# One pipeline of 16 attention units in place of 12 and 4, with the second kind's transposed operands in free ring places

## The reference

```python
o_n = nsa_mixer(q_n, k_c, v_c, k_s, v_s, k_w, v_w, g_n, ...)   # 8 query heads in 2 key groups, 3 gated branches
o_m = moba_mixer(q_m, k_m, v_m, cos, sin)                      # 8 heads with keys of their own
o = jnp.concatenate([o_n, o_m], axis=-1) @ w_o[l]
```

## Time and profile before

| | us |
|---|---|
| median of 3 runs | 2891.91 (2890.43 to 2893.74) |
| the profiled execution | 2889.56 |
| span of the profiled execution | 2887.8 |
| mean granted PE clock | 0.979 |
| PE, PEld, DVE, ACT, POOL busy in the span | 2796.0, 2382.1, 1772.7, 1317.6, 172.1 |

### The profile page before, as it was taken

The page is one execution under the profiler, slowest core; times in us unless marked ns, Lnnn a source line. Parts: engine busy times, 40 slices in busy tenths (PEclk is TensorE's granted clock), DMA queues, the critical chain, the costliest instruction groups (busy, mean ns, idle before and its releaser), DMA issues.

```text
span 2887.8 us, 35130 instructions
## 1 busy us (share of the span) xinstructions
PE 2796.0 (97%) x13510; PEld 2382.1 (82%) x13510; DVE 1772.7 (61%) x2028; ACT 1317.6 (46%) x1658; POOL 172.1 (6%) x132
## 2 busy tenths in 40 slices
PE   8998999999999999999999999998889999999998
PEld 8998978888878888888888889876778888888886
DVE  4466568676557787865555564444684755644445
ACT  5454234454434545434454444344455444344443
POOL 0001620000000000000000002630000000000000
PEclk9998999999999999999999999897999999999999
DMA  8453038877647777775555556450455766755553
GB/s 283 150 171 119 0 124 290 286 274 266 217 161 255 281 273 261 283 252 199 190 188 197 185 179 202 160 190 1 154 201 186 267 227 218 275 188 179 190 187 119
DMA packets 293266, 579.60 MB, mean 201 GB/s; under 512 B 9168, under 2 KB 46192, under 8 KB 292112
## 3 DMA queue, kind: packets, MB, share of 16 engines
q1 hardware_dynamic: 291296, 566.08, 57.5%
q0 software_dynamic: 1120, 8.57, 0.8%
q10 hardware_dynamic: 720, 3.15, 0.3%
HBM read 575.66 MB, written 2.10 MB: 200 GB/s over the span
## 4 chain that ended last, share of the span: by engine, by line
PE 94%; DVE 3%; ACT 1%; issue 1%; DMA 0%; POOL 0%; SPq 0%; DVEq 0%; ACTq 0%
PE GP L853 28%; PE GP L855 28%; PE GP L854 28%; PE TA L830 2%; PE TB L476 2%; PE TB L830 1%; PE GP L462 1%; PE TA L1210 1%; PE TB L872 1%; DVE small L553 0%; PE GP L1056 0%; PE TA L1056 0%; PE GP L1046 0%; DMA x<-in_x 0%; PE TA L1244 0%
## 5 line engine op out<-in xcount | busy, mean ns | idle before, releaser
L1754 DVE TENSOR_TENSOR wlo<-raw,whi 128x1024 fp32r<-128x1024 f32 (+2 forms) x904 | 1086.9, 1214 | 853.6 <-ACT whi L1286 844.7
L1286 ACT CAST whi<-raw 128x1024 fp32r<-128x1024 f32 (+2 forms) x904 | 924.8, 1029 | 1206.7 <-PE GP L855 1158.5
L853 PE MATMUL GP<-whi,hhi 128*128 128x512 f32 (+2 forms) x1792 | 689.4, 385 | 3.1 <-DVE hlo L578 1.6
L855 PE MATMUL GP<-whi,hlo 128*128 128x512 f32 (+2 forms) x1792 | 681.3, 380 | 0.0
L854 PE MATMUL GP<-wlo,hhi 128*128 128x512 f32 (+2 forms) x1792 | 681.2, 380 | 0.0
L853 PEld LDWEIGHTS GP<-whi,hhi 128*128 128x128 f32 x1792 | 338.7, 189 | 54.7 <-issue 3.0
L855 PEld LDWEIGHTS GP<-whi,hlo 128*128 128x128 f32 x1792 | 338.1, 189 | 52.0
L854 PEld LDWEIGHTS GP<-wlo,hhi 128*128 128x128 f32 x1792 | 338.4, 189 | 51.1 <-issue 1.0
L853 PE MATMUL GP<-whi,bhi 128*128 128x512 f32 x704 | 276.6, 393 | 0.2 <-DVE blo L1814 0.2
L1742 DVE SCALAR_TENSOR_TENSOR ada_acc<-raw,csig,ada_acc 128x512 f32<-128x512 f32 x360 | 270.2, 751 | 10.2
L855 PE MATMUL GP<-whi,blo 128*128 128x512 f32 x704 | 274.3, 390 | 0.0
(11 more groups left out here) (410 smaller groups left out, 2667.7 us busy)
## 6 DMA issues: line engine op xcount, KB each, us to landing
raw<-in_w_up SPq DMA_DIRECT2D x108, 1024.0 KB, 5.3
raw<-in_w_down SPq DMA_DIRECT2D x108, 1024.0 KB, 5.1
raw<-in_w_ada SPq DMA_DIRECT2D x96, 1024.0 KB, 5.1
raw<-in_w_gate SPq DMA_DIRECT2D x44, 1024.0 KB, 5.1
raw<-in_w_in SPq DMA_DIRECT2D x48, 856.0 KB, 4.6
raw<-in_w_xkv SPq DMA_DIRECT2D x32, 1024.0 KB, 5.5
raw<-in_w_in SPq DMA_DIRECT2D x24, 1024.0 KB, 4.9
raw<-in_w_in SPq DMA_DIRECT2D x24, 864.0 KB, 4.5
```

Source lines behind the costliest of these rows:

```text
L853: pe.matmul(o, ahi[:, kt, t], whi[r][:, k, 0:q.width], start=first, stop=False)
L855: m = pe.matmul(o, alo[:, kt, t], whi[r][:, k, 0:q.width], start=False, stop=last)
L1286: nc.scalar.copy(whi[(2 * g + s) % NRING][:, :, 0:q.width], raw[j % NSLOT][:, 2 * s:2 * s + 2, 0:q.width])\
L1754: TTo(wlo[r][:, :, 0:q.width], raw[j % NSLOT][:, 2 * s:2 * s + 2, 0:q.width], whi[r][:, :, 0:q.width].bitcast(F32), ALU.subtract).then_inc ...
```

## The change

The 12 and 4 units become one list of 16, run as one pipeline `natt`; stage `matt` is gone. The three blocks of n2 are transposed at points of `w_in2c` (behind its third, fifth and seventh unit), and ACT copies them in hooks. The second kind gets operands of its own, `qTm` and `kTm`, of 8 KB per partition each, which lie over `whi2`, `whi3` and `wlo2`, `wlo3`. Its four blocks are transposed behind `w_in2c` (two) and behind the transposes of units 0 and 1 (one each). So that the ring places are free, `w_in2c` splits only the first unit of `w_oa` ahead (`lead=1`), and the second is split when attention is over.

```diff
-                   for i, (n, u, g) in enumerate((("xatt", 0, 0), ("natt", 2, 8), ("matt", 14, 12)))}
+                   for i, (n, u, g) in enumerate((("xatt", 0, 0), ("natt", 2, 8)))}
...
+        qTm = nc.alloc_sbuf_tensor_at("qTm", [P, 8, T], F32, offset=ring0 + 4096 * 2)
+        kTm = nc.alloc_sbuf_tensor_at("kTm", [P, 8, T], F32, offset=ring0 + 4096 * (NRING + 2))
...
-                                   qk=[[(qT2[:, h, hf * P:hf * P + P], kT2[:, h, 0:nk * P])] for h in hs],
+                                   qk=[[(qTm[:, h, hf * P:hf * P + P], kTm[:, h, 0:nk * P])] for h in hs],
...
-        def attention_pe(pe, turn, nm_, us):
+        def attention_pe(pe, turn, nm_, us, behind={}, ahead={}):
...
+                if i in ahead:
+                    ahead[i]()
...
                     if ngroup >= 2:
                         pe.wait_ge(*N(nm_, "lo", ngroup - 1))
+                    elif nm_ == "natt":
+                        pe.wait_ge(*N("m2", "c", 4))
...
                 m.then_inc(N(nm_, "t")[0], 1)
+                if i in behind:
+                    behind[i]()
                 if i:
                     values(i - 1)
...
-            product(PH["w_in2c"], hhi, hlo, lambda u: (S("norm_lo"), 40))
-
+            def later_turn(g):
+                if g == 0:
+                    pe.wait_ge(S("rope_done"), 2)
+                elif g == 1:
+                    pe.wait_ge(S("cmp_oc"), 2)
+                else:
+                    pe.wait_ge(*N("n2", "c", 1))
+                turn_in2(turn, "n2", later[g])
+
+            def block_turn(g):
+                if g == 0:
+                    pe.wait_ge(*N("n2", "c", 3))
+                elif g == 1:
+                    pe.wait_ge(*N("n2", "c", 2))
+                else:
+                    pe.wait_ge(*N("m2", "c", g))
+                turn_in2(turn, "m2", blocks[g])
+
+            product(PH["w_in2c"], hhi, hlo, lambda u: (S("norm_lo"), 40),
+                    points={(0, 2): lambda: later_turn(0), (1, 0): lambda: later_turn(1), (1, 2): lambda: later_turn(2)})
+            pe.wait_ge(S("rope_done"), 4)
+            block_turn(0)
+            block_turn(1)
             for e in range(2):
                 pe.wait_ge(S(f"evac{e}"), 1 + PH["w_in2c"].ev1)
...
-            turn_in2(pe, turn, "n2")
-            attention_pe(pe, turn, "natt", nsa_units())
-            turn_in2(pe, turn, "m2")
-            attention_pe(pe, turn, "matt", moba_units())
-            pe.wait_ge(*N("natt", "lo", 4))
+            attention_pe(pe, turn, "natt", nsa_units() + moba_units(), behind={0: lambda: block_turn(2), 1: lambda: block_turn(3)},
+                         ahead={12: lambda: pe.wait_ge(*N("m2", "c", 4))})
...
                 for j in range(LEAD):
-                    if nxt is not None:
+                    if nxt is not None and j < lead:
                         split_hi(*nxt, j)
...
+            for g, at in enumerate((5, 7, 9)):
+                hooks[at] = hooks.get(at, []) + [lambda it, g=g: turn_in2_act(act, "n2", later[g], g + 1)]
+            phase(PH["w_in2c"], hooks, lead=1)
+            turn_in2_act(act, "m2", blocks[0], 1)
+            turn_in2_act(act, "m2", blocks[1], 2)
+            attention_act(act, "natt", nsa_units() + moba_units(),
+                          behind={i: lambda i=i: turn_in2_act(act, "m2", blocks[2 + i], 3 + i) for i in range(2)})
+            split_hi(PH["w_oa"], 0, 1)
...
-            phase(PH["w_in2c"], {})
+            phase(PH["w_in2c"], {}, lead=1)
...
-            attention_dve(dve, link, "natt", nsa_units())
-            dve.wait_ge(*N("m2", "c", 4))
-            dve.sem_inc(N("matt", "go")[0], 1)
-            attention_dve(dve, link, "matt", moba_units())
+            attention_dve(dve, link, "natt", nsa_units() + moba_units())
+            split_lo(PH["w_oa"], 0, 1)
```

More of the change, by code:

```diff
@@ L488, in attention_pe @@
                     pe.wait_ge(*N(nm_, "c", i))
+                elif nm_ == "natt":
+                    pe.wait_ge(*N("m2", "c", 1))
                 for kb in range((u["L"] + P - 1) // P):
@@ L496, in attention_pe, with attention_act @@
             values(len(us) - 1)
-        def attention_act(act, nm_, us):
+        def attention_act(act, nm_, us, behind={}):
             ng = 0
@@ L596, in GP_flat, with turn_in2, turn_in2_act @@
             return _F()
[L600 to L612, removed]
-                    pe.wait_ge(*N("natt", "lo", 4))
[L614 to L623, removed]
+        later = [(qT2, 0, [0, 128, 256, 384], TA), (qT2, 4, [512, 640, 768, 896], TB),
+                 (kT2, 0, [KV0 + 512, KV0 + 640, KV0 + 1024, KV0 + 1152], TA)]
+        blocks = [(qTm, 0, [QM0 + P * i for i in range(4)], TA), (qTm, 4, [QM0 + P * i for i in range(4, 8)], TB),
+                  (kTm, 0, [QM0 + 1024 + P * i for i in range(4)], TB), (kTm, 4, [QM0 + 1024 + P * i for i in range(4, 8)], TB)]
+        def turn_in2(turn, nm_, part):
+            _, _, cs, tp = part
+            for f, c in enumerate(cs):
+                for h in range(NH):
+                    m = turn(tp[:, f * T + h * P:f * T + h * P + P], p2[:, h, c:c + P])
+            m.then_inc(N(nm_, "t")[0], 1)
+        def turn_in2_act(act, nm_, part, n):
+            dst, a, _, tp = part
+            act.wait_ge(*N(nm_, "t", n))
+            nc.scalar.copy(dst[:, a:a + 4, :], v(tp, T)).then_inc(N(nm_, "c")[0], 1)
         raws = [(x, 0, hhi, hlo), (memt, 2, mhi, mlo), (x, 1, hhi, hlo), (x, 3, bhi, blo)]
@@ L1245, in gate_row @@
                     .then_inc(S("gate_mm"), 1)
-            product(PH["w_oa"], hhi, hlo, lambda u: N("matt", "lo", 4),
+            product(PH["w_oa"], hhi, hlo, lambda u: N("natt", "lo", 8),
                     points={divmod(i + 1, 4): lambda i=i: gate_row(0, i) for i in range(4)})
-            product(PH["w_ob"], hhi, hlo, lambda u: N("matt", "lo", 4))
+            product(PH["w_ob"], hhi, hlo, lambda u: N("natt", "lo", 8))
             for g in range(6):
@@ L1287, in split_hi, with body @@
                         .then_inc(S("hi_done"), 1)
-            def body(q, it, nxt, hooks):
+            def body(q, it, nxt, hooks, lead=LEAD):
                 g = 0
@@ L1305, in body, with phase @@
                         f(it)
-            def phase(q, hooks, peel=False, last={}, ahead=True, head={}):
+            def phase(q, hooks, peel=False, last={}, ahead=True, head={}, lead=LEAD):
+                assert lead == LEAD or q.n == 1
                 i0 = order.index(q)
@@ L1318, in phase @@
                     with loop(act, m) as it:
-                        body(q, it, (q, it + 1), hooks)
+                        body(q, it, (q, it + 1), hooks, lead)
                 if not same:
                     both = {at: hooks.get(at, []) + last.get(at, []) for at in hooks.keys() | last.keys()}
-                    body(q, q.n - 1, (nq, 0) if nq is not None else None, both)
+                    body(q, q.n - 1, (nq, 0) if nq is not None else None, both, lead)
             def raw_square(s, hs=(0, 1)):
@@ L1780, in body, with phase @@
                     ada_out()
-            def phase(q, hooks, peel=False, links=0, last={}, ahead=True, head={}):
+            def phase(q, hooks, peel=False, links=0, last={}, ahead=True, head={}, lead=LEAD):
+                assert lead == LEAD or q.n == 1
                 i0 = order.index(q)
```

4 lines of the change are left out of this document (removed).

## The result

The changed kernel takes 2872.84 us (median of 4, 2870.88 to 2874.52), the kernel before 2891.17 (median of 4): ratio 0.9938, 95% interval 0.9925 to 0.9950, so 18.3 us less. 2874.0 was forecast, with 2867 to 2881 as the range.

What follows compares the result with a forecast made beforehand. PE was taken as the bound, busy 2796.0 of 2887.8 us, with this stage bound by the PE, DVE, ACT chain. Front 1.5, seam 15.8 and clock gave gains of 13.0 to 23.6; 18 was taken: 2874 us, range 2867 to 2881.

Steps and rivals of the forecast that it cites:

- The front: From `w_in2c` to the first exponentials: three blocks go under the product; 1.5 us gained, bounds 2.1 gain to 0.4 loss.
- The seam: Values of unit 11 to transposes of the second new unit: only unit 15's scores remain, 17.6 us become 1.8, removing 15.8.
- The tail: Transposes of the second new unit to `w_oa`: 13.8 us, same order of work, about 3 us wait at unit 14; nothing gained.
- low piece of the old tail: Half-clock work in the tail before `w_oa` that need not come again; 1.7 us given back.
- The clock: PE's granted clock around the seam decides the rest; a shorter low stretch than before was assumed, total gain 18 us.
- two ends: Clock at the seam: low as before from unit 11's transposes gives 13.0 us gain; full gives 21.9, or 1.7 more.
- price of 0.45 us for a low microsecond: Within the half-clock rival: each added microsecond of half clock in the stage loses 0.45 us.
- Half clock all along: Rival: clock stays at 0.50 from behind the front to `w_oa`, which starts 12 us later; 2904 us; chance 0.04.
- Full clock through the seam: Rival: denser work keeps PE at full clock at the seam; gain 21 to 24 us, 2868 to 2871; chance 0.2.
- The start of `w_oa`: Second unit split behind attention, ready 2.5 us into `w_oa`, needed after 5.4; no cost.
- Both margins: At `w_oa`: the late `w_ada` load is used 16.5 us in, and the `w_o` loads come 2.5 us later; no cost.

Runs made afterwards that it cites:

- first profile: The changed kernel as first measured and profiled, against the kernel before: 2872.84 us, ratio 0.9938.
- filled kernel before: The kernel before with discarded matmuls of constants put into nine of PE's waits for a division, against the kernel before: 2885.20 us, ratio 0.9980.
- second profile: The changed kernel measured and profiled again without any edit, against the kernel before: 2871.36 us, ratio 0.9930.
- seam alone: The changed kernel with the three n2 blocks transposed behind `w_in2c` instead of inside it, against the kernel before: 2872.22 us, ratio 0.9940.
- six `pT`: The changed kernel with six buffers `pT` instead of three, the new ones in `p2`; against the kernel before: 2866.80 us, ratio 0.9925.
- changed kernel with filling: The changed kernel with discarded matmuls of constants in PE's waits at seven units, against the kernel before: 2867.41 us, ratio 0.9919.

## Why the prediction was right

**The front.** Forecast: `w_in2c` 2.6 us longer on PE, scores 2.1 us earlier, exponentials 1.5. Measured from the base: the last matmul of `w_in2c` starts at 44.86 instead of 42.14 (2.7), scores at 46.83 instead of 49.14 (2.3), exponentials 1.51 earlier. That the two blocks behind units 0 and 1 fit into gaps at nothing holds at full clock only. From the first exponentials to the transposes of unit 6 it took 23.0 us in the first profile, with nothing low, and 23.0 in the filled kernel before, which has no blocks there (3.4 low). With 6.8 low us there it took 25.6 in the second profile and in the seam alone, against 24.1 before with 10.2 low: at half clock PE has no gap left, and the blocks cost 1.4 us or more. Ahead of the scores they cost 5.0 us, so their place is still worth more than the 1.9 of the forecast. What the front brings to the time is small: 1.3 us alone and 0.9 as the last piece, neither told apart from nothing.

**The seam.** Forecast: 17.6 us become 1.8. Measured: 2014.57 - 2013.01 = 1.6. This is the step that carries the result, and the seam alone gave it.

**The tail.** Forecast: 13.8 us, with a wait of about 3 us at unit 14. Measured: 2028.68 - 2014.57 = 14.1, wait 3.08. The reason given was only half of it: behind the copy of unit 12 the cast of the values of unit 11 waits for the same end, as six `pT` showed. The term was right, its holder incomplete. The 1.7 us that the forecast gave back for a low piece of the old tail did not come: the new tail has such a piece too (3.4 us, the last line of the windows below).

**The clock.** The forecast put the low stretch behind unit 10 and took a middle between two ends. In the profile after it lay elsewhere (windows of PE: length, busy, granted clock):

```profile
1975.80:1985.90 10.10, 10.10 (x39) 0.51 0.00 1
1986.10:2002.80 16.70, 13.04 (x93) 1.00 0.00 1
2002.90:2006.20 3.30, 3.30 (x11) 0.50 0.00 0
2006.50:2019.90 13.40, 10.32 (x72) 1.00 0.00 1
2020.10:2023.20 3.10, 3.10 (x16) 0.50 0.02 5
```

It hit units 5 to 7, and the transposes of unit 11, 2.6 us ahead of the kernel before at unit 6, were 0.9 us later from the base than before (101.19 against 100.30). The stretch from them to the values took 4.87 us instead of 3.13. The values of unit 11 ran at full clock, 6.08 instead of 10.98. The account of the 18.0 us is thus -0.9 - 1.7 + 4.9 + 16.0 - 0.3. The forecast had, in the same places, 1.3; 0.1 to 3.2 lost; 0 to 4.9; 14.2 to 15.8; and 0 to 1.7. So the seam, by far the largest term, was right, and the values of unit 11 gave the full 4.9 us. That the sum fell on 18 is partly luck: 2.2 us lost at units 5 to 7, which no term had, stand against the 4.9. In the second profile of the same kernel the low time lay elsewhere (10.2 us) and the stage was 20.5 us shorter than before. The price of 0.45 us for a low microsecond fits the 0.33 to 0.49 found above. Middle and range were the right use of the clock; its place was not to be had.

**The rivals.** Half clock all along did not come: low stretches got fewer (17.1, 10.2 and 13.7 us in joined pipelines against 34.1). Full clock through the seam nearly came (3.4 us low there). Its gain, 21 to 24 us, would have asked for full clock everywhere: the changed kernel with filling has that, and is 22.4 us below the kernel before in the stage. On the rule of the Trainium skill that activity releases the throttle (TensorE: Matmul & The Clock Gate, What's actually happening) the filled kernels agree, with clocks of 0.96 and 1.00 for 0.82 and 0.89. Against it stand the values of unit 11 before, at 0.50 for 11 us without a gap.

**The start of `w_oa`.** No wait, 55.12 of 55.20 us busy. SP and DVE of the changed kernel, beside the earlier trace rows:

```profile
2031.21 0.37 SPq L692 DMA_DIRECT2D raw<-in_w_ada  x1
2033.97 3.13 SPq L692 DMA_DIRECT2D raw<-in_w_o  x2
...
2045.14 3.11 DVE L1765 SCALAR_TENSOR_TENSOR ada_acc<-raw,csig,ada_acc 128x512 f32<-128x512 f32 x4
```

The load of `w_ada` is issued 2.5 us into `w_oa` and used 13.9 us later, the loads of `w_o` 5.3 us in (2.5 before). Both margins held.

## What to carry to other kernels

Where two pipelines of the same three engines follow each other, the seam costs the drain, the preparation and the filling of the second; look for places for the operands that let them be one list, and count what stands between the same two steps before and after. Transposes that prepare a stage belong into gaps where PE waits anyway: in a row ahead of the stage each pays the round over the copy (5.0 us for two here). A gap measured at full clock can be gone at half clock, so price such work at both. Before a gain is given to an edit, compare the low time of the two profiles: of 4.1 to 6.7 us with six `pT`, 1.6 were the edit's. When a wait hangs on an item in another engine's queue, the item behind it may wait for the same event, so move both before expecting the wait to go.

## What was not expected of the hardware

Discarded matmuls in PE's waits raise the granted clock of a thin stage from 0.82 to 0.96, worth 4.5 us (ratio 0.9980, 0.9971 to 0.9989) in the kernel before, although the stretch from unit 10 to unit 11, which holds three of them, became 3.5 us longer.

The stretch ahead of the stage, the same code in all kernels, ended at 1893.90 to 1902.11 us in the profiles. In identical code the granted clock differed between profiles, as 0.83 (before) and 0.90 (changed, again) from 250 to 300 us. From the start of `w_oa` to the end it was 842.4 to 843.5 us. So single executions can't be compared within some 8 us by their totals, but stages counted from a base in the same trace can, with their low time beside them. What sets off a fall at one place in one execution and not in the next stays open.
